# Routed expert weights: six loads of 512 KB per expert become three of 1 MB

## What is computed

```python
def swiglu(h, w_gate, w_up, w_down):
    return (jax.nn.silu(h @ w_gate) * (h @ w_up)) @ w_down

    # router: 8 of 64 experts for each token, weights scaled by 2.5
    ys = lax.map(expert_block, (xs, blk_e)).reshape(n_rows, d)   # 128 rows at a time, one expert each
    ys = ys * row_w[:, None].astype(ys.dtype)
    return jax.ops.segment_sum(ys, row_tok, num_segments=t_tok)
```

## Time and profile before

| | |
|---|---|
| runs | 2861.36, 2848.2, 2853.92 us |
| median | 2853.92 us |
| the profiled execution, its own time | 2842.91 us |
| its span, from the first to the last instruction | 2841.2 us |
| mean granted TensorE clock | 0.976 |
| PE, DVE, ACT, POOL busy, share of the span | 94%, 63%, 43%, 47% |
| `route` | from 0 to about 1223 us |
| loop of the routed blocks | from about 1251 to 2683 us |

### The profile page before, as it was taken

One profiled execution on the slowest core, in us unless ns is written; L12 is line 12 of the kernel. 1 busy time (PEld: TensorE's weight loads), 2 busy tenths in 40 slices (PEclk: granted clock), 3 DMA queues, 4 the chain that ended last, 5 costly groups with the idle time before them and its releaser, 6 DMA issues.

```text
span 2841.2 us, 50420 instructions
## 1 busy us (share of the span) xinstructions
PE 2683.9 (94%) x11902; PEld 2177.7 (77%) x11903; DVE 1799.3 (63%) x2519; ACT 1218.4 (43%) x1738; POOL 1330.1 (47%) x1116
## 2 busy tenths in 40 slices
PE   7999999999999999559999999999999999999996
PEld 6888888788878887447777777877777788777875
DVE  5534555555555555557667766676776767667576
ACT  3233223223223232135555655555555555556432
POOL 3000002200230033557777777777777778777612
PEclk9999999999999999779999999999999999999998
DMA  8223333432343235159989989898998998898875
GB/s 305 93 96 115 130 104 98 132 134 98 101 137 137 97 104 170 60 172 267 265 248 268 286 244 256 235 261 246 275 265 246 269 257 255 244 253 251 219 232 188
DMA packets 169918, 554.82 MB, mean 195 GB/s; under 512 B 30145, under 2 KB 35889, under 8 KB 169873
## 3 DMA queue, kind: packets, MB, share of 16 engines
q1 hardware_dynamic: 95776, 344.42, 34.7%
q0 software_dynamic: 65888, 195.67, 29.1%
q10 hardware_dynamic: 8208, 14.16, 1.5%
HBM read 434.97 MB, written 119.18 MB: 195 GB/s over the span
## 4 chain that ended last, share of the span: by engine, by line
PE 34%; issue 7%; POOL 4%; DVE 3%; ACT 2%; DMA 2%; another core or an unknown queue 2%; ACTq 2%; DVEq 1%; POOLq 1%
PE ps_gu L1466 8%; PE ps_gu L1468 7%; PE ps_gu L1467 7%; PE ps_y L1468 3%; PE ps_y L1466 3%; PE ps_y L1467 3%; POOL xs L1412 3%; PE ps_h L1513 1%; ACT expert_hi L1543 1%; DMA acc_odd<-y,sidx 1%; DVE expert_lo L1648 1%; ACTq L1365 1%; DVEq L1673 1%; POOLq L94 0%
## 5 line engine op out<-in xcount | busy, mean ns | idle before, releaser
L1412 POOL DMA_INDIRECT xs<-h_dram,gidx x656 | 829.1, 1264 | 323.9 <-issue 191.7
L1466 PE MATMUL ps_gu<-expert_hi,xl 128*128 (+1 forms) x1392 | 570.8, 410 | 20.2 <-DVE xl L1664 18.9
L1467 PE MATMUL ps_gu<-expert_lo,xh 128*128 (+1 forms) x1392 | 555.3, 399 | 0.0
L1468 PE MATMUL ps_gu<-expert_hi,xh 128*128 (+1 forms) x1392 | 555.2, 399 | 0.0
L1648 DVE TENSOR_TENSOR expert_lo<-expert_raw,expert_hi 128x1024 f32 (+1 forms) x390 | 459.8, 1221 | 101.4 <-ACT expert_hi L1543 70.6
L917 DVE TENSOR_TENSOR ul<-raw,uh 128x1024 fp32r<-128x1024 f32 x186 | 227.9, 1225 | 402.9 <-ACT uh L741 380.4
L1543 ACT ACTIVATE expert_hi<-expert_raw 128x1024 f32 (+1 forms) x390 | 390.5, 1052 | 53.9 <-PEq L1517 42.8
L93 POOL TENSOR_SCALAR rstd<-mean 128x1 f32<-128x1 f32 x49 | 15.8, 323 | 843.5 <-ACT junk L760 828.6
L504 PE MATMUL ps_t<-hh,ul 128*128 128x512 f32 x1024 | 402.0, 393 | 3.1 <-DVE wgl L1146 3.1
L506 PE MATMUL ps_t<-hh,uh 128*128 128x512 f32 x1024 | 399.6, 390 | 0.0
L505 PE MATMUL ps_t<-hl,uh 128*128 128x512 f32 x1024 | 399.5, 390 | 0.0
(11 more groups left out here) (263 smaller groups left out, 3796.4 us busy)
## 6 DMA issues: line engine op xcount, KB each, us to landing
expert_raw<-experts SPq DMA_DIRECT2D x396, 512.0 KB
raw<-units SPq DMA_DIRECT2D x192, 512.0 KB
xs<-h_dram,gidx POOLq DMA_INDIRECT x656
h_dram<-h ACTq DMA_DIRECT2D x17, 512.0 KB
acc_odd<-h POOLq DMA_DIRECT2D x17, 512.0 KB, 14.8
acc<-x SPq DMA_DIRECT2D x4, 2048.0 KB, 8.1
expert_raw<-acc_odd SPq DMA_DIRECT2D x16, 512.0 KB, 6.6
expert_raw<-x POOLq DMA_DIRECT2D x14, 512.0 KB, 3.7
```

The source lines that it names most:

```text
L1412: nc.gpsimd.indirect_dma_start(xs[s][:, g * DQ:(g + 1) * DQ], None, h2_quarters, bass.IndirectOffsetOnAxis(ap=gidx[s][:, g:g + 1], axis=0) ...
L1466: nc.tensor.matmul(out_, sl, vh, start=first, stop=False)
L1467: nc.tensor.matmul(out_, sh, vl, start=False, stop=False)
L1468: return nc.tensor.matmul(out_, sh, vh, start=False, stop=last)
```

## The change

Two pieces that lie side by side are loaded by one DMA, everywhere where expert weights are loaded. SP waits once for both rooms (for the count that the second piece's split gives), issues one DMA of 1 MB, and one semaphore tells of both. There are three semaphores `piece_in` in place of six; ACT waits for `piece_in[p // 2]`.

```diff
-        piece_in = [sem(f"piece_in{p}") for p in range(PIECES)]
+        piece_in = [sem(f"piece_in{p}") for p in range(PIECES // 2)]
...
-            for p in range(PIECES):
-                sp.dma_start(expert_raw[:, p, :], experts[0][:, p, :]).then_inc(piece_in[p], 16)
+            for p in range(0, PIECES, 2):
+                sp.dma_start(expert_raw[:, p:p + 2, :], experts[0][:, p:p + 2, :]).then_inc(piece_in[p // 2], 16)
...
-                for p in range(PIECES):
-                    wait(sp, piece_ready, (e - 1) * PIECES + p + 1)
+                for p in range(0, PIECES, 2):
+                    wait(sp, piece_ready, (e - 1) * PIECES + p + 2)
...
-                    sp.dma_start(raw[:, p, :], src[:, p, :]).then_inc(piece_in[p], 16)
+                    sp.dma_start(raw[:, p:p + 2, :], src[:, p:p + 2, :]).then_inc(piece_in[p // 2], 16)
...
-            for p in range(PIECES):
+            for p in range(PIECES // 2):
                 sp.wait_ge(piece_in[p], 16 * (NE + 2))
...
-                    act.wait_ge(piece_in[p], (e + 1) * 16)
+                    act.wait_ge(piece_in[p // 2], (e + 1) * 16)
```

## The result

The changed kernel took 2878.34 us (median of four runs, 2874.72 to 2883.96), the kernel before 2851.06 us beside it (four runs, 2838.91 to 2861.36). The ratio is 1.0102, with a 95% interval of 1.0073 to 1.013: slower by about 27 us, and clear of noise. The profiled execution after took 2877.64 us, its span is 2876.0 us, 34.8 us more than before.

A forecast was written before the change was run, and what follows sets the result against it. PE was taken to set the pace, with the DMA engines close behind. Issues saved, issue times and mixture start at 0 plus packets at 7.7 us, on 2853.9 us, gave 2861.6 us, 0.3% slower; range 2840 to 2890 us.

The forecast's parts named there:

- rival B: Blocks opening an expert: scatters contend in full behind 8 KB packets, 33 us slower, 2887 us; chance 0.24.
- What bounds the kernel, and the path: Routed blocks: PE sets the pace, DMA close behind; late scatters delay ACT, splits and `hid`, 13 PE stalls, 19.7 us.
- Issues saved: SP's sequencer: 198 fewer loads save 65 us of issue time, worth 0 as SP only waits between them.
- Issue times moved: Weight loads: pieces 0, 2 and 4 go later but still land before ACT needs them; cost 0.
- Packets: DMA queues: 8192 B packets delay each scatter by 0.6 us on the mean, 1.5 at most; +7.7 us.
- How much reaches PE: PE's stalls for `hid`: 13 scatters whose lateness reaches PE, 0.6 us each, 7.7 us.
- The clock: PE after stalls: half-clock drops of 1.7 us each, five of them counted in the slower rival, none in the sum.
- Start of the mixture: First two row tiles' gathers beside expert 1's load: taken as 0, bounded by -2 and +3 us.
- (A): DMA queues: packets stay 4096 B or scatters don't notice, so nothing before PE moves; 2854 us, chance 0.20.
- (C): DMA engines: later, fewer loads leave them free for scatters and gathers, stalls and three clock drops go; 2829 us, chance 0.12.
- (D): Weights late: piece 2 lands behind its use, 65 experts at 1 us, 65 us; 2919 us, chance 0.02.

The follow-up runs named there:

- e7: Kernel before, with GpSimd issuing the scatter ahead of the block's four gathers; 2765.69 against 2803.0 us, ratio 0.9863.
- e8: Changed kernel, with GpSimd issuing the scatter ahead of the block's four gathers; 2767.86 us, ratio 0.9866 to the kernel before.
- e1: Kernel before, issuing at the changed kernel's moments but as two 512 KB DMAs back to back, 4096 B packets; 2834.07 us, ratio 1.0104.
- e5: Kernel before, only piece 2 held back to go with piece 3, still 512 KB DMAs; 2842.89 against 2803.0 us, ratio 1.0143.
- e2: Changed kernel with 256 unused bytes behind each piece in DRAM, so packets are 4096 B; 2836.09 us, ratio 1.0104 to the kernel before.
- a0: Changed kernel, unchanged, rerun on the chip of the experiments; 2844.36 us, ratio 1.0144 to the kernel before.
- triples: Changed kernel with three pieces per DMA, two loads of 1.5 MB per expert; 2778.64 us, ratio 0.9911 to the kernel before.
- e6: Kernel before, only piece 3 held back to go with piece 4, 2.7 us later; 2766.59 us, ratio 0.9872.
- padded triples: Loads of three pieces, 1.5 MB, with 256 unused bytes behind each piece in DRAM, 4096 B packets; 2788.96 us, ratio 0.9946 to the kernel before.
- e3: Kernel before, each piece loaded by two 256 KB DMAs, 2048 B packets, same moments of issue; 2786.0 us, ratio 0.9936.
- b0: Kernel before, unchanged, profiled on the chip of the experiments; profiled execution 2812.04 us.

## Why the prediction was right in its sign and short in its size

The forecast was 2861.6 us, 7.7 us slower; measured were 2878.3 us, 27.3 us slower than the median beside it. The time lies in the range (2840 to 2890). The number came near rival B (33 us), and so did its path, but not its cause. That the sign came out right is therefore in part luck: the whole of the 7.7 us stood on packets of twice the length, and kernels with the old length lose as much.

- **What bounds the kernel, and the path**: right. The chain scatter, `output` on ACT, splits, `hid`, PE of rows 5 to 7 is the one that grew, and taking the scatter's wait away (e7, e8) takes the whole loss away, as far as the runs can tell.
- **Issues saved, 0**: right. e1 issues all six and loses as much.
- **Issue times moved, 0**: this is the step that failed. I compared each new moment with the use of the same piece, and there was room, as said: ACT never waited for a pair. The loss came from elsewhere: I did not compare it with the other transfer for which somebody waits soon. Piece 2 moved from 1911.12 to 1914.22 in rows 8; by the timeline, a scatter was issued at 1914.05. e5 makes this move alone and its ratio is 1.0143, as large as that of the change. In every kernel with this move the scatter's packets begin 1.1 to 1.4 us later than in the kernel before (3.0 us after the issue).
- **Packets, 7.7 us**: the packets did become 8192 B (141,404 in all and 116,016 under 8 KB, where I had 141,400 and 116,000). But the whole of the price stood on them, and e1 and e2 lose as much with 4096 B. I had a scatter take up to 1.5 us longer between its packets; from the sixth to the 116th it takes 2.6 us after where it took 3.2. What the length itself does is small and has no one sign: 0.4% at the edge of the intervals for pairs (a0 against e1 and e2), the other way for triples.
- **How much reaches PE**: under-sized. I took 0.6 us for each of 13 scatters. ACT's waits before `sidx` rose by 47.4 us, and PE's wait for `hid` by 18.1 net where I had 7.7; the stalls behind a late scatter alone grew by about 34 us, from 13 to 24 of them.
- **The clock**: I put no clock drops into the forecast, only five into rival B. PE's busy time rose by 19.4 us, more than its waits for `hid` did net. Without stalls they go as well: the mean granted clock over the span is 0.982 in e6 and 0.974 in `a0`.
- **Start of the mixture, 0 within -2 and +3 us**: this fits. DVE's first two waits for rows are 2.16 and 2.93 us in the profile after, 5.09 together, where they were 2.82 and 2.28, 5.10 together: one shorter and one longer, as I had reasoned.
- **The rivals**: (A) fell with the packets and the time. (C) fell; "the load starts later and engines are free" was nonetheless a true mechanism, only that pairs put the free stretch in the wrong place: e6 has it. (D) fell for pairs; it shows in the padded triples (18.8 us).

The Trainium skill's rule on turns between queues ("DMA: Bandwidth & Descriptors", "Queues, rings and completion order") was my ground for pricing by packet length. The runs don't refute it, but two kernels with half the packet length and the same moments lost as much, so it doesn't carry the price. The Trainium skill's rule of at least 1 MiB per DMA (the same page, "Rules for kernel authors") brought nothing here: e2 with 1 MB and e1 with 512 KB, at the same moments and packets, are both at 1.0104.

Open remains why e3, with packets of 2048 B at the moments of before, gains 0.6%. Shorter packets that let the scatter through sooner would fit; then longer ones should cost more than a0 against e1 shows, and in triples they don't cost at all; and the scatter's sixth packet starts 2.8 us after the issue in e3, hardly sooner than the 2.9 of `b0`. A burst that ends sooner, ahead of the scatter, might turn the sign there. That is argued, not shown. That e5 costs as much as the change, though pieces 0 and 4 keep their moments, fits its scatters, which begin as late as there (4.1 us). Why it lies even a little above e1 and e2 is open. So is why GpSimd's queue gets so little while a fresh load runs: that its packets stand ready and wait is not shown.

## What to carry to other kernels

When a transfer is merged or moved, don't only ask whether its own consumer still gets it in time. List what else is in flight at the new moment, and who waits for that: on shared engines a bulk load with 6 us to spare can hold up a small transfer with none. The cheapest mend is often to give the urgent transfer another place: here to issue the scatter ahead of the gathers, or to hold one piece back by 2.7 us until the scatter is on its way, made the kernel 1.3 to 1.4% faster, where no transfer became smaller or larger.

## What the runs showed of the hardware

- A fresh load of 1 MB took nearly all of the engines: in 2040:2042 of the kernel after q1 had 95.2% and q0 0.02 MB, with a scatter issued at 2038.84. I had expected the two to alternate. On the mean over the openings, the scatter's sixth packet starts 3.0 us after the issue in the kernel before, 4.1 to 4.4 us where 1 MB is queued a us ahead of it, and 2.2 us where the load comes behind it (e6).
- A packet of q1 with 8192 B took 0.31 us and one with 4096 B 0.16 us (medians in the profile after), so the longer packets moved hardly more bytes per us. The 0.19 us of the prediction is a mean over one us in which the engines were 97.6% busy with q1.
- Stalls of PE cost twice. In the kernel after, the 4.89 us stall was followed by a window of 7 us with a granted clock of 0.51; over the span 18.1 us more of stalls went with 19.4 us more of busy time. In the kernels without stalls the clock in the routed blocks stood at 1.00.
- Chips differ by more than the change: the kernel before took 2851 us on one and 2802 to 2806 us on three others. On the first, ACT waited 68.3 us for `hth` with the remark remote, on the others this row is missing; in the kernel after it is 13.3 us on the first, so it isn't steady there either. PE waited 43.6 us for `hid` there and 22.7 us in `b0`. Why is not known.
